# Output projection of a hybrid mixer layer: Strassen's products over all sixteen row tiles, with sixteen weight sums made early, and one scale of the last pair moved ahead of a weight split

## The reference, cut to what matters

```python
h = rms_norm(x, norm_g)                                  # x: 1024 tokens x 2048, f32
proj = jnp.einsum('bsd,de->bse', h, w_in)                # 2048 -> IN_WIDTH columns
...
mixed = jnp.concatenate([
    out_a.astype(h.dtype) * jax.nn.silu(az),             # dilated windows, 12 heads of 64
    out_b.astype(h.dtype) * jax.nn.silu(bz),             # forgetting attention, 8 heads of 64
    out_c.astype(h.dtype) * jax.nn.silu(cz)], axis=-1)   # gated linear attention, 4 heads
return x + jnp.einsum('bse,ed->bsd', mixed, w_out)       # 2048 x 2048 output projection
```

## Time and profile before

| | |
|---|---|
| median of 3 runs | 2040.43 us (2038.71 to 2040.92) |
| profiled execution | 2044.43 us |
| its span (first to last instruction) | 2042.7 us |
| TensorE busy | 2008.2 us, 98% |
| VectorE, ScalarE, GpSimd busy | 1121.9, 891.1, 503.1 us |
| mean granted clock of TensorE | 0.998 of full speed |

### The profile page before, as it was taken

The page is one execution under the profiler, slowest core; times in us unless marked ns, Lnnn a source line. Parts: engine busy times, 40 slices in busy tenths (PEclk is TensorE's granted clock), DMA queues, the critical chain, the costliest instruction groups (busy, mean ns, idle before and its releaser), DMA issues.

```text
span 2042.7 us, 28729 instructions
## 1 busy us (share of the span) xinstructions
PE 2008.2 (98%) x10024; PEld 1690.6 (83%) x10024; DVE 1121.9 (55%) x1733; ACT 891.1 (44%) x1504; POOL 503.1 (25%) x400
## 2 busy tenths in 40 slices
PE   6999999999999999999999999999999999999998
PEld 5788888888888888888888888888888887788787
DVE  7611456465445555555555555555555657613797
ACT  7311343444454445445454445445444556411242
POOL 0000343251531212222221212222122210002565
PEclk9999999999999999999999999999999999999999
DMA  7322424324332222222222222323232274466646
GB/s 236 81 72 71 116 68 109 100 82 103 94 98 78 61 85 78 87 67 72 87 72 85 64 89 79 107 58 98 83 97 71 85 249 145 134 200 222 237 155 196
DMA packets 204559, 223.20 MB, mean 109 GB/s; under 512 B 17336, under 2 KB 143336, under 8 KB 203328
## 3 DMA queue, kind: packets, MB, share of 16 engines
q1 hardware_dynamic: 187760, 191.73, 31.8%
q10 hardware_dynamic: 16720, 30.45, 4.0%
HBM read 173.35 MB, written 48.78 MB: 109 GB/s over the span
## 4 chain that ended last, share of the span: by engine, by line
PE 85%; DVE 7%; ACT 2%; DMA 2%; issue 2%; POOL 1%; SPq 0%; DVEq 0%; ACTq 0%; POOLq 0%
PE acc L2266 19%; PE acc L2268 19%; PE acc L2267 19%; PE pv L2504 4%; PE turned L2489 4%; PE scores L2481 2%; PE scores L2478 2%; DVE w_lo L1724 1%; DVE act_lo L2209 1%; DMA w_raw<-in_w_in_dram 1%; PE acc L2616 1%; DVE fast_out L2222 1%; PE acc L2553 1%; PE acc L2555 1%; PE acc L2554 1%
## 5 line engine op out<-in xcount | busy, mean ns | idle before, releaser
L2266 PE MATMUL acc<-act_hi,w_hi 128*128 128x512 f32 x1848 | 737.1, 399 | 2.5 <-DVE w_lo L1724 1.9
L2268 PE MATMUL acc<-act_hi,w_lo 128*128 128x512 f32 x1848 | 722.0, 391 | 0.0
L2267 PE MATMUL acc<-act_lo,w_hi 128*128 128x512 f32 x1848 | 720.7, 390 | 0.0
L2268 PEld LDWEIGHTS acc<-act_hi,w_lo 128*128 128x128 f32 x1848 | 346.9, 188 | 75.4
L2266 PEld LDWEIGHTS acc<-act_hi,w_hi 128*128 128x128 f32 x1848 | 347.5, 188 | 69.5 <-DVE w_lo L1724 4.8
L2267 PEld LDWEIGHTS acc<-act_lo,w_hi 128*128 128x128 f32 x1848 | 347.7, 188 | 65.2
L1724 DVE TENSOR_TENSOR w_lo<-w_raw,w_hi 128x512 fp32r<-128x512 f32 x223 | 199.4, 894 | 358.6 <-ACT w_hi L1239 358.3
L1545 ACT ACTIVATE prob<-prob,neg_max 128x128 f32<-128x128 f32 (+7 forms) x160 | 124.0, 775 | 251.1 <-DVE neg_max L2035 251.1
L1159 POOL TENSOR_TENSOR vz<-raw 32x512 f32<-32x512 f32 x72 | 85.6, 1189 | 468.3 <-ACT sq L1492 465.6
L1239 ACT ACTIVATE w_hi<-w_raw 128x512 fp32r<-128x512 f32 x223 | 139.1, 624 | 137.2 <-PE acc L2268 110.1
L2051 DVE TENSOR_TENSOR pt_lo<-turned,pt_hi 128x1024 fp32r<-128x1024 f32 (+1 forms) x120 | 114.9, 957 | 146.9 <-ACT pt_hi L1553 146.3
(11 more groups left out here) (427 smaller groups left out, 3007.0 us busy)
## 6 DMA issues: line engine op xcount, KB each, us to landing
w_raw<-in_w_in_dram SPq DMA_DIRECT2D x240, 256.0 KB, 2.9
proj_scratch<-stage ACTq DMA_DIRECT2D x116, 256.0 KB, 2.1
w_raw<-in_w_out_dram SPq DMA_DIRECT2D x64, 256.0 KB, 3.5
raw<-proj_scratch SPq DMA_DIRECT2D x20, 512.0 KB, 3.4
logit_bias<-in_w_out_dram SPq DMA_DIRECT2D x35, 256.0 KB, 4.6
act_lo<-mixed_scratch SPq DMA_DIRECT2D x7, 1024.0 KB, 8.6
t_raw<-in_w_out_dram SPq DMA_DIRECT2D x28, 256.0 KB, 3.7
extra_raw<-in_w_out_dram SPq DMA_DIRECT2D x23, 256.0 KB, 3.5
```

Of the source, the lines that this page charges most:

```text
L2266: pe.matmul(acc, hi, xh, start=first, stop=False)
L2267: pe.matmul(acc, hi, xl, start=False, stop=False)
L2268: mm = pe.matmul(acc, lo, xh, start=False, stop=end)
```

## The change

1. The two sets of Strassen's row tiles become 8 and 8: tiles 0 to 7, and 8, 10 to 15, 9. The left runs for groups 2 and 3 go; one left item stays, tile 9 for column group 0, and it is now the first run of the stage. The stage has 1 + 7 x 8 = 57 items and 24 + 672 = 696 matmuls.
2. The products are put in another order. Products 2 and 6 are accumulated on top of products 0 and 4 in the same PSUM banks (`FAST_ON_TOP`), so merges fall from 72 to 48. Merges of a run are spread over six steps.
3. The 16 weight sums of products 1 and 2 (`SUMMED_SOONER`) are made by GpSimd near the start of the program, beside the last six groups of `C_ALONE`: SP loads two pieces of `w_out` into `g_wide`, GpSimd adds or subtracts, SP stores the sum to a new DRAM scratch (`summed`), from which it is loaded in the fast stage. There are two places, and SP does this between two `load_quarter` calls, so a wait in it stands ahead of later loads of `w_raw`.
4. Row tiles 8 and 9 of `mixed` are now stored to DRAM too (`store_pair(LAST - 1)` at early load 7, tile 9 in column group 1), as the row sums need them; `load_gate(LAST)` and `load_res(1)` wait until these stores have landed.
5. In the last pair, at slot 28, the scale of the last query block stands ahead of the split of a weight piece on VectorE.

```diff
+LATE_FIRST = 28
...
-FAST_ROWS = (list(range(7)), [7] + list(range(LAST + 1, KT)))
-FAST_LEFT = (LAST - 1, LAST)
+FAST_ROWS = (list(range(LAST - 1)), [LAST - 1] + list(range(LAST + 1, KT)) + [LAST])
...
-FAST_WEIGHTS = (((0, 1), ALU.subtract, (1, 1)), ((1, 0), ALU.subtract, (0, 0)), ((0, 0), ALU.add, (1, 1)),
-                ((0, 0), None, None), ((1, 1), None, None), ((0, 0), ALU.add, (0, 1)), ((1, 0), ALU.add, (1, 1)))
-FAST_ROW_SUMS = (None, None, ((0, 0), ALU.add, (1, 1)), ((1, 0), ALU.add, (1, 1)), ((0, 0), ALU.add, (0, 1)),
-                 ((1, 0), ALU.subtract, (0, 0)), ((0, 1), ALU.subtract, (1, 1)))
-FAST_INTO = (((1, 0, ALU.add), (1, 1, ALU.add)), ((0, 1, ALU.add), (0, 0, ALU.add)),
-             ((0, 0, ALU.add), (1, 1, ALU.add)), ((0, 1, ALU.add), (1, 1, ALU.subtract)),
-             ((1, 0, ALU.add), (0, 0, ALU.subtract)), ((1, 1, ALU.add),), ((0, 0, ALU.add),))
-FAST_RUNS = [("product", 0), ("product", 1), ("left", 0), ("left", 1), ("left", 2)] + [("product", q) for q in range(2, 7)]
-LEFT_ROWS = (FAST_LEFT, FAST_LEFT, FAST_LEFT[1:])
-LEFT_COLS = (FAST_CGS[0] * HALF, FAST_CGS[1] * HALF, 0)
+FAST_WEIGHTS = (((0, 1), ALU.subtract, (1, 1)), ((1, 0), ALU.subtract, (0, 0)), ((0, 0), ALU.add, (0, 1)),
+                ((0, 0), None, None), ((0, 0), ALU.add, (1, 1)), ((1, 1), None, None), ((1, 0), ALU.add, (1, 1)))
+FAST_ROW_SUMS = (None, None, ((1, 0), ALU.subtract, (0, 0)), ((1, 0), ALU.add, (1, 1)), ((0, 0), ALU.add, (1, 1)),
+                 ((0, 0), ALU.add, (0, 1)), ((0, 1), ALU.subtract, (1, 1)))
+FAST_ON_TOP = (2, 6)
+SUMMED_SOONER = (1, 2)
+SOONER = [(q, j) for q in SUMMED_SOONER for j in range(FAST_K)]
+SOONER_AT = 2
+FAST_INTO = (((1, 0, ALU.add),), ((0, 1, ALU.add), (0, 0, ALU.add)), ((1, 1, ALU.add),),
+             ((0, 1, ALU.add), (1, 1, ALU.subtract)), ((1, 1, ALU.add),), ((1, 0, ALU.add), (0, 0, ALU.subtract)),
+             ((0, 0, ALU.add),))
+FAST_RUNS = [("left", 2)] + [("product", q) for q in range(7)]
+LEFT_ROWS = {2: (LAST,)}
+LEFT_COLS = {2: 0}
...
+MERGE_STEPS = 6
...
-ROW_SUM_STEP = [first + j for first in (9, 16, 23, 30, 37) for j in range(FAST_K)]
+ROW_SUM_STEP = [first + j for first in (4, 12, 20, 28, 36) for j in range(FAST_K)]
...
+    return weight_terms(q, j)[:1 if q in SUMMED_SOONER else 2]
+def weight_terms(q, j):
...
-    return FAST_WEIGHTS[q][1] if kind == "product" else None
+    return FAST_WEIGHTS[q][1] if kind == "product" and q not in SUMMED_SOONER else None
...
-            out += own[2 * (n - e - 1):2 * (n - e)]
+            out += [own[i] for i in range(len(own)) if e + 1 + i * MERGE_STEPS // len(own) == n]
...
-        merged_into = [fast_out[0], fast_out[1], res]
+        merged_into = [res, fast_out[1], fast_out[0]]
...
-            with sp.Fori(AHEAD, C_ALONE) as s:
-                for kq in range(4):
-                    load_quarter(s, kq, COL_CQ + s * P)
+            def load_sooner(i):
+                if i == 0:
+                    sp.wait_ge(x_turned, 4 * NT)
+                elif i >= 2:
+                    sp.wait_ge(small_saved, 16 * i)
+                for to, (k, col) in zip(sooner[i % 2], weight_terms(*SOONER[i])):
+                    sp.dma_start(to, w_out_k[:, k, col:col + HALF]).then_inc(row_summed, 16)
+            def store_sooner(i):
+                sp.wait_ge(t_summed, i + 1)
+                sp.dma_start(summed[i * P:(i + 1) * P, :], sooner[i % 2][0]).then_inc(small_saved, 16)
+            for n in range(4 * (C_ALONE - AHEAD)):
+                load_quarter(AHEAD + n // 4, n % 4, COL_CQ + (AHEAD + n // 4) * P)
+                if 0 <= n - SOONER_AT - 1 < len(SOONER):
+                    store_sooner(n - SOONER_AT - 1)
+                if 0 <= n - SOONER_AT < len(SOONER):
+                    load_sooner(n - SOONER_AT)
+            for i in range(4 * (C_ALONE - AHEAD) - SOONER_AT - 1, len(SOONER)):
+                store_sooner(i)
+            sp.wait_ge(small_saved, 16 * (len(SOONER) + 1))
...
                 load_early_rows(n)
+                if n == 7:
+                    store_pair(LAST - 1)
...
+                    sp.wait_ge(mixed_saved, 16 * LAST)
                     load_gate(LAST, last_column)
...
-            def load_fast_residual(c, t):
-                cols = slice(FAST_CGS[c] * HALF, (FAST_CGS[c] + 1) * HALF)
-                sp.dma_start(fast_out[c][:, t, :], x_rows[t * P:(t + 1) * P, cols]).then_inc(x_in[c], 16)
+            def load_fast_residual(t):
+                cols = slice(FAST_CGS[1] * HALF, (FAST_CGS[1] + 1) * HALF)
+                sp.dma_start(fast_out[1][:, t, :], x_rows[t * P:(t + 1) * P, cols]).then_inc(x_in[1], 16)
...
             def load_partial(t):
+                sp.dma_start(fast_out[0][:, t, :], partial[t * P:(t + 1) * P, :]).then_inc(x_in[0], 16)
+            def load_first_residual(t):
+                cols = slice(FAST_CGS[0] * HALF, (FAST_CGS[0] + 1) * HALF)
...
-                sp.dma_start(res[:, t, :], partial[t * P:(t + 1) * P, :]).then_inc(res_in[t], 16)
+                sp.dma_start(res[:, t, :], x_rows[t * P:(t + 1) * P, cols]).then_inc(res_in[t], 16)
...
             def load_rows_again(th, kh, j):
...
-                sp.wait_ge(quarter_done, 3 * (GROUPS + AHEAD) + EARLY - len(ROUNDS) + OUT_ORDER.index(k) + 1)
+                if k == LAST:
+                    sp.wait_ge(out_ready, 2 * NT)
+                else:
+                    sp.wait_ge(quarter_done, 3 * (GROUPS + AHEAD) + EARLY - len(ROUNDS) + OUT_ORDER.index(k) + 1)
...
-                    .then_inc(mix_in[0 if th == kh else 1 + kh], 16)
+                    .then_inc(mix_in[2 * kh + (th != kh)], 16)
...
-                for to, (k, col) in zip((t_ones[slot], t_twos[slot]), weight_loads(n)):
-                    sp.dma_start(to, w_out_k[:, k, col:col + HALF]).then_inc(terms_in[slot], 16)
+                kind, q = FAST_RUNS[run_of(n)[0]]
+                if kind == "product" and q in SUMMED_SOONER:
+                    i = SOONER.index((q, run_of(n)[1]))
+                    sp.dma_start(t_ones[slot], summed[i * P:(i + 1) * P, :]).then_inc(terms_in[slot], 16)
+                else:
+                    for to, (k, col) in zip((t_ones[slot], t_twos[slot]), weight_loads(n)):
+                        sp.dma_start(to, w_out_k[:, k, col:col + HALF]).then_inc(terms_in[slot], 16)
...
+            sp.wait_ge(o_done, LAST + 3)
+            sp.dma_start(mixed[LAST * P:(LAST + 1) * P, :], vz[:]).then_inc(mixed_saved, 16)
...
+            sp.wait_ge(mixed_saved, 16 * PAIRS)
             load_res(1)
...
-                            load_fast_residual(1, t)
+                            load_fast_residual(t)
...
-                    load_rows_again(1, 1, kk - 12)
+                    if kk == 12:
+                        load_rows_again(0, 0, FAST_K - 1)
+                    load_rows_again(1, 0, kk - 12)
...
-                        load_fast_residual(0, t)
+                        load_partial(t)
...
+            load_rows_again(1, 0, 4)
...
-            load_rows_again(1, 1, 5)
+            load_rows_again(1, 0, 5)
...
-            load_rows_again(1, 1, 6)
+            load_rows_again(1, 0, 6)
...
+            load_rows_again(1, 0, 7)
...
-                    load_rows_again(1, 0, n - 8)
+                    load_rows_again(1, 1, n - 8)
...
-                        load_partial(t)
+                        load_first_residual(t)
...
-                if 28 <= n < 32:
-                    for t in range(2 * (n - 28), 2 * (n - 28) + 2):
+                if 20 <= n < 24:
+                    for t in range(2 * (n - 20), 2 * (n - 20) + 2):
...
-                if 45 <= n < 49:
-                    save_merged(0, 4 + n - 45)
+                if 48 <= n < 52:
+                    save_merged(0, 4 + n - 48)
...
+            for i, (q, _j) in enumerate(SOONER):
+                pool.wait_ge(row_summed, 32 * (i + 1))
+                pool.tensor_tensor(sooner[i % 2][0], sooner[i % 2][0], sooner[i % 2][1], FAST_WEIGHTS[q][1]).then_inc(t_summed, 1)
...
                     steps(slot)
+                    if slot == LATE_FIRST:
+                        late(slot)
...
                         split_next(n + EARLY_AHEAD)
-                    late(slot)
+                    if slot != LATE_FIRST:
+                        late(slot)
...
                         split_next(n + EARLY_AHEAD)
...
-                    pe.matmul(banks[b], hi, t_his[slot], start=first, stop=False)
-                    pe.matmul(banks[b], hi, t_los[slot], start=False, stop=False)
-                    mm = pe.matmul(banks[b], lo, t_his[slot], start=False, stop=at_end)
+                    pe.matmul(banks[b], hi, t_his[slot], start=first and not on_top, stop=False,
+                              skip_group_check=on_top)
+                    pe.matmul(banks[b], hi, t_los[slot], start=False, stop=False, skip_group_check=on_top)
+                    mm = pe.matmul(banks[b], lo, t_his[slot], start=False, stop=at_end, skip_group_check=on_top)
```

(35 more changed lines are left out.)

## The result

The change made the kernel slower: 2044.69 us median (2042.57 to 2046.60, 15 runs) against 2040.40 us for the kernel before (2038.70 to 2042.23, 15 runs). The ratio is 1.0020, with a 95% interval of 1.0013 to 1.0028. The forecast was 2034.3 us, with a range that ended at 2040.5.

The account below looks back on a forecast made before the run. TensorE's own work was taken as the bound (busy 2008.2 of 2042.7 us). Terms -5.25 + 0.2 - 1.05 = -6.1 us gave 2038.3 against the profiled execution, 2034.3 us against the median; range 2032.3 to 2040.5.

Parts of the forecast that it names:

- The early sums: Near the program's start, 16 weight sums on idle GpSimd: 0 us taken, with 0 and 6.2 us for the range.
- the first rival: In the groups that stand alone, SP falls back and TensorE waits 2 to 6.2 us: 2036.3 to 2040.5; chance 0.21.
- L: Early sums: time from the second load's issue to GpSimd's start, 3.72 us alone, 4.57 with stores, put near 4.1.
- The cover: Early sums: how late a w_raw load may be before TensorE waits, 9.2 us after landing, halves and pair.
- 15c - 94.9: Early sums: TensorE's wait after 15 cycles of c us each; nothing up to c = 6.33.
- 15c - 85.7: Early sums: how late SP's load 18, the last behind a pair, comes after 15 cycles of c us.
- The second rival: SP falls back until slower than before, needing a cycle of 7.05 us: 2044.5 us or more; chance 0.05.
- The fast stage: Stage from the left item's first matmul to the last product's: 164.95 to 159.7 us, a gain of 5.25 us.
- VectorE and GpSimd: In the fast stage, 8 steps of doubled GpSimd work again: small wait of 0.2 us, bounds 0 and 1.0.
- The third rival: VectorE and GpSimd become the fast stage's bound, TensorE waits 1 to 3 us: 2035.3 to 2037.3; chance 0.09.
- The scale: Last query block: reciprocal and scale ahead of the weight split start 1.05 us sooner, bounds 0 and 1.46.
- Stores of tiles 8 and 9: Last pair and column group 1: 512 KB more in a full queue, taken as 0, bounds 0 and 1.5 us.

Follow-up runs that it names:

- twelve in a row: Changed kernel with 12 early sums in consecutive quarters, three quarters without one, then the other four; 2039.31 us, ratio 0.9995 to the kernel before.
- with pauses: Changed kernel with the early sums made in three of each four quarters instead of 16 quarters in a row; 2034.00 us, ratio 0.9970 to the kernel before.
- the other queue: Changed kernel with the 16 early-sum stores issued by GpSimd on its own queue, no longer by SP; 2034.47 us, ratio 0.9968 to the kernel before.
- the first experiment: Changed kernel with each early sum's store issued by SP two quarters behind its pair of loads, no longer one; 2040.11 us, ratio 0.9997 to the kernel before.

## Why the prediction was wrong, point by point

**The early sums: wrong, and the step that failed the forecast.** "I take 0" stands in the sum for them, and they cost 10 to 11 us. The chain of causes stood in the text, as the first rival: the store waits for GpSimd, the next `w_raw` load stands behind it, the cycle is longer than a quarter, SP falls back, TensorE waits for `w_lo` near 180 to 200 us. The bounds of the cycle were right too, 5.9 to 6.8 us; it measured 6.71. Three sizes in it were wrong or missing.

- *L.* "puts L between the two rows, near 4.1" is the sentence that failed. The measured cycle gives L = 6.71 - 0.85 - 1.29 - 0.05 = 4.52 us, next to the upper row. Read from the rows, from the second load's issue to GpSimd's start, it is 4.4 us at the median, and 5.3 and 5.5 us in the two cycles in which ScalarE issued two stores beside the pair (160.94 to 168.38 and 188.10 to 195.77, 7.4 and 7.7 us long). The lower row is of a pair with nothing ahead; here a store always is. In a product with 15, the 0.4 us of L are 6 us. The sum itself was also a little off: by its own terms L = 4.57 us gives c = 6.76 and a wait of 6.5 us, not 6.2.
- *The cover.* I had 2.8 us of landing plus 1.55 for the pair ahead. At the median the pieces did land near that, in 4.5 us. But those issued at 162.28 and 189.44, beside ScalarE's stores, took 6.1 and 6.4 us, and TensorE's two long waits, 2.3 and 2.6 us, are for these two; those stores had no term. That takes 2.1 us off the cover of 9.2, and the 5.8 us of 15c - 94.9 become 7.9. Behind its last wait TensorE is in fact 9.5 us late (11.0 less the 1.5 of slow matmuls that follow). Of the rest, 1.1 us is SP: the load of 189.44 is 16.1 us later than the same one of the kernel before, where 15c - 85.7 gives 15.0. The run with twelve in a row bears out the smaller cover. The load before:

```profile
173.34 0.37 SPq L656 DMA_DIRECT2D w_raw<-in_w_in_dram  x1
```

- *The clock.* The 16 matmuls at 1.2 GHz, in two stretches behind waits of 2.3 and 2.6 us, took 3.1 us more than at 2.4 GHz, and the sum had no term for it; I had priced a wait of TensorE at its length. What it cost is probably less than 3.1. The first stretch lies ahead of waits whose end SP set, so it may only have made them shorter; that is argued, but the kernel before with the early sums, with no such stretch there, has its mark as late to 0.1 us. The executions give the price: of the 15 of the changed kernel, seven had a mean granted clock of 0.997 and a median of 2045.10 us, the other eight 0.999 or more and 2043.50. So the low clock goes with 1.6 us, and at the full clock the change is still 3.1 us slower than the kernel before.

The second rival had the right sign with 0.05, and its threshold was too high: it asked for a cycle of 7.05 us, while 6.71 was enough.

**The fast stage: right.** 159.5 us measured, 159.7 without waits and 159.9 with one predicted. No wait at a border of runs.

**VectorE and GpSimd: right, 0.2 us too much.** I expected a wait of 0.2 us at the sixth product; there is none. The experiment without early sums shows how near the bound is: 11.1 us with 16 more double steps. The third rival named the right mechanism for that kernel, but it does not act in this one.

**The scale: right.** 1.05 us predicted, 1.1 in the rows, 1.4 in the medians (of which up to 0.9 may be the wait for `pt_lo`, 1.5 us with the scale behind and 0.6 with it in front, in one execution each).

**Stores of tiles 8 and 9: right at 0,** as far as the wait shows: 2.8 us for `pt_lo` before, 1.7 after, 0.6 with pauses, 1.1 to 1.7 in the other runs of the changed kernel. The kernel before with the early sums, whose last pair is the old one, has 1.8, so a part of the difference is from one execution to the next, and the change need not have made it shorter.

**Not in the sum:** from the last matmul's start to the end of the span it is 4.4 us (2043.4 - 2039.00), and was 5.4 (2042.7 - 2037.28 in the earlier trace rows). It is 4.3 to 4.4 us in all seven kernels with the new fast stage and 5.5 in the kernel before with the early sums, so the change brings this 1.0 us. I had no term for it; which part of the stage's new end brings it is open.

With the head free the forecast's number holds: 2034.0 us by pauses, 2034.5 by the other queue, against 2034.3. That it is met to 0.3 us is in part luck. The fast stage (5.4 us), the scale (1.1) and the end (1.0) add up to 7.5 us, and 6.4 are measured; the head with pauses ends 1.0 us later than that of the kernel before (229.75 against 228.75), which is within what these marks scatter. Two terms that I did not have, 1.0 us each, about cancel.

With the head as it is, the mark stands 10.1 us behind that of the kernel with pauses (239.82 and 229.75): 2034.0 + 10.1 = 2044.1, against 2044.7 measured. Open is why the clock fell in some executions and not in others, and about half a microsecond of SP's and TensorE's delay.

## What to carry to other kernels

A queue that waits for a result in each step has a cycle of its own: add up issue, landing, work and issue, and compare it with the consumer's period. If it is longer, the number of steps in a row decides, and each doubtful tenth of a microsecond is multiplied by that number; take the landing from a row with the same transfers ahead of it, not from the middle between two. Then move the wait off the queue that feeds the bottleneck, or leave pauses in which the queue catches up: here either turned a loss of 4.3 us into a gain of about 6. When a wait is moved, look at what the new wait is for: a store issued right behind loads lands behind them.

## What the hardware showed beyond that

- A 256 KB store from SP landed in 2.0 us (median) when SP's queue had been idle, in 3.4 us when one 256 KB load had been issued 0.4 us ahead of it (101.17 and 101.59 in the changed kernel), and in 4.9 us (median of the first experiment) when three had been issued in the 1.3 us ahead of it. The Trainium skill, page "DMA: Bandwidth & Descriptors", section "Queues, rings and completion order", says that an increment lands only after every earlier write of the same DMA engine; by that rule a store cannot be seen before the loads that are ahead of it, and these rows agree.
- With a share of 0.98 the DMA engines moved 338 GB/s. In the changed kernel, from 1675 to 1680 us, they moved 415 GB/s at a share of 1.03. A share near 1 is no fixed rate: the 1.55 us that I had worked out from 338 GB/s would be 1.26 at 415.
- A GpSimd addition of two 128x512 tiles takes 1.29 us alone and 1.74 us where VectorE and GpSimd are both at work nearly without a gap, so the slowdown that the earlier trace rows show for VectorE goes both ways (the 1.74 is from the kernel without early sums).
